# Layer 0's backward gates three feed-forward blocks later, and the last pass's second output half token block by token block

## The chip, the cores and the metric

One Trainium2 chip, eight of its cores. Each core runs the same program on one of the eight sequences of the batch; the cores exchange nothing. The time of a run is the device time of its slowest core in microseconds (us).

## The reference

A bidirectional encoder with two layers on x of shape 8 x 4096 x 1024, followed by a root-mean-square norm. Per layer:

```
h = rmsnorm(x); z = h @ w_in                       # u, v, lru_x, lru_gate, gate_A, gate_B
y_a = gelu(u) * (w_s @ layernorm(gelu(v)) + b_s)   # per chunk of 128 positions
xc  = conv4(lru_x)                                 # taps -1, 0, +1, +2
for each direction:                                # forward and backward
    r, i = sigmoid(xc @ w_r + b_r), sigmoid(xc @ w_i + b_i)   # 8 heads of 128 x 128
    a = sigmoid(L) ** (8 r);  h_t = a_t h_(t-1) + sqrt(1 - a_t^2) * i_t * xc_t
y_b = (h_fwd + h_bwd) * gelu(lru_gate)
x = x + (sigmoid(gate_A) * y_a + sigmoid(gate_B) * y_b) @ w_out
h = rmsnorm(x); g, u = split(h @ w_ffn_in)
x = x + (silu(g) * u) @ w_ffn_out                  # inner width 2816
```

## The kernel before, in words

The 4096 tokens are eight tiles of 512 tokens (`TT`), a tile is four blocks of 128 tokens (`NS`), the model width is eight blocks of 128 (`KC`), and the inner feed-forward width is 22 blocks of 128 (`FC`). Matrix products are in bf16 with 512 columns a matmul, sums in float32 PSUM. There are three passes over the tiles.

- **First pass**, tiles 0 to 7: layer 0's projections, gating branch and forward recurrence.
- **Second pass**, tiles 7 to 0: for tile j the rest of layer 0 (backward recurrence, merge, output projection, feed-forward), and in the same step, for tile j+1, the projections, the gating branch and the backward recurrence of layer 1.
- **Last pass**, tiles 0 to 7: the rest of layer 1 (forward recurrence, merge, output projection, feed-forward) and the final norm.

A step of the second pass goes over TensorE in this order: merge projections and layer 1's conv input; output projection; layer 1's v, u and gate_A projections with its eight gate pairs; then feed-forward input and output. The feed-forward input is 22 blocks, `("FI", f, 0)` and `("FI", f, 1)`, eight matmuls each (`ffn_in`, L1186). Between these blocks stand the eight gate pairs `("R0", c)` of layer 0's backward recurrence for the next tile (`gates`, L711: one matmul for r and one for i). The feed-forward output (`ffn_out`, L1208) is two halves of 512 output columns, `nb`. Each half needs six streamed weight chunks `q` of up to four rows of blocks, and four PSUM banks, one for each block `s` of 128 tokens.

What a gate pair needs: `xgates` casts the conv output `xm`, reloaded from HBM by `xcload` (L922 in layer 0, L908 in layer 1), to bf16 (`xcb`, L972, ScalarE). The product goes to one of the two PSUM banks of the ring "gate", and ScalarE's tanh writes it to `ra` or `ib` (L714). `xm`, `ra` and `ib` are single buffers of eight blocks for both layers. So layer 0's gates wait until layer 1's recurrence is through with them: `xm` may be loaded when L743 has read it, and `ib` may be written when the scans (L746) are done and `hbstore` (L914) has stored it to HB. Load and store are in two halves of four blocks, 1 MB each. `recur` then makes exp (L727), square (L733), square root (L738), product (L743) and scan.

Weights come from a bf16 copy WB in HBM in chunks of up to 512 KB (L1093) through a ring `wr` of 11 buffers. A chunk's buffer is free when its last matmul is done. All these DMAs are issued by SyncE (SPq in the rows), in its fixed order; an entry that waits holds up those behind it.

In the last pass the residual rows `xr` (512 KB for each 128 tokens) have a ring of five buffers, and a tile uses four. After `ffn_out` VectorE adds the product to `xr` (L1213), ScalarE squares it (L1547), GpSimd takes the root, VectorE scales it (L1551) and SyncE stores it to `out` (L1554). The next tile's output projection (L1162) adds to rows loaded by L1519 into the buffers so freed; the first of its four is free beforehand.

The order: TensorE's is written by hand (`seq`, lists of tokens, sorted by key). The order on the other engines is made by a list scheduler (`Sched.order`) from assumed costs and due times. So a moved token on TensorE also moves work elsewhere. PSUM banks are handed out in TensorE's order: five to "main", two to "gate", one to "t".

Of the kernel before, what the change touches and what calls it, by code (L numbers as in the profile page):

```python
# [14 lines left out]
KC = 8  # L15
# [5 lines left out]
NS = TT // 128  # L21
# [431 lines left out]
def build_program():  # L453
    nc = bass.Bass("TRN2", target_bir_lowering=False)
    stack = contextlib.ExitStack()
    with stack:
        _build(nc, stack)
    return nc
# [9 lines left out]
def _build(nc, stack):  # L468
# [819 lines left out]
    def seq(g, tokens):  # L1288
        return {t: (g, float(i)) for i, t in enumerate(tokens)}

    def fseq(extra):

        r = []
        for f in range(FC):
            r += [("FI", f, 0), ("FI", f, 1)] + [t for a, t in extra if a == f]
        return r + [("FO", nb, q, s) for nb in range(2) for q in range(6) for s in range(NS)]

    def aseq():
# [64 lines left out]
    for i in range(NT + 1):  # L1363
# [3 lines left out]
        tok = []  # L1367
# [22 lines left out]
        if j >= 0:  # L1390
            extra = [(n, t) for n, t in enumerate(late)]
            if i == 0:
                extra += [(2 + 2 * n, ("CON", n)) for n in range(5)]
            if j > 0:
                extra += [(int(7 + 1.7 * c), ("R0", c)) for c in range(KC)]
            tok += fseq(extra)
        else:
            tok += late
# [92 lines left out]
    for j in range(NT):  # L1491
        g = G3 + 1 + j
        nxt = j + 1 < NT
        tok = [("OP", s, nb) for s in range(NS) for nb in range(2)]
        extra = []
# [13 lines left out]
            tok += [("T2", s) for s in range(NS)]  # L1509
        if j + 2 < NT and j > 0:  # L1510
            extra += [(int(4 + 1.7 * c), ("R", c)) for c in range(KC)]
        tok += fseq(extra)
        if j == 0:
            for c in range(KC):
                tok.insert(tok.index(("FO", c // 6, c % 6, NS - 1)) + 1, ("R", c))
# [17 lines left out]
        for f in range(FC):  # L1533
            ffn_in(lambda t: K_["FI", f, t], hTb[0], hTb[1], sfi, f)
            if f in gat:
                c = gat[f]
# [45 lines left out]
```

How the kernel before makes its waits and increments, by code:

```python
            def body(eng, prog=self.prog[e], last=(self.final if e == "sp" else ())):  # L430
                for fn, waits, inc in prog:
                    for sem, v in waits:
                        eng.wait_ge(sem, v)
                    ins = fn(eng)
                    if inc is not None:
                        ins.then_inc(inc[0], inc[1])
                for sem, v in last:
                    eng.wait_ge(sem, v)
```

## Time and profile before

| | us |
|---|---|
| median of 3 runs | 4124.24 |
| the runs | 4122.54, 4124.24, 4664.74 |
| the profiled execution, its own time | 4136.46 |
| its span, core 1 (slowest) | 4134.9 |
| TensorE busy | 3747.6 (91%) |
| VectorE busy | 2467.1 (60%) |
| ScalarE busy | 2210.1 (53%) |

The profile is of one execution of its own, on core 1 unless another core is named. In timeline rows, the first number is the start in us from the beginning of the span, the second the time from the first start to the last end of the merged instructions, and in brackets stands the idle time of the engine before them and what ended it. A matmul of 512 columns starts every 0.216 us when nothing holds it up (64 in 13.8 us), though its row says 379 ns.

### The profile page before, as it was taken

To read this page: it belongs to the slowest core of one execution; us is meant where nothing else is said; L and a number is where in the kernel's file an instruction comes from. 1 tells how busy PE (TensorE), PEld (TensorE's weight loads), DVE (VectorE), ACT (ScalarE), POOL (GpSimd) and SP (SyncE) were. 2 spreads that over 40 slices of the span, in tenths; PEclk is the share of its full clock that TensorE was granted. 3 is DMA by queue.
4 is the path that set the end of the run, shared out by engine and by line. 5 is a ranking of instruction groups with operands and counts; after the bars stand their busy time and mean duration, and the time that the engine had idled before them with its cause. 6 is when DMAs were issued, how large, how long until landed. Compare 5 with 4: busy or idle time off the path is not lost.

```text
span 4134.9 us, 56456 instructions; the slowest of 8 cores (4063.2 to 4134.9 us)
## 1 busy us (share of the span) xinstructions
PE 3747.6 (91%) x17826; PEld 1706.4 (41%) x17826; DVE 2467.1 (60%) x3625; ACT 2210.1 (53%) x3252; POOL 350.3 (8%) x594
## 2 busy tenths in 40 slices
PE   5788888798999998999999999868999999999988
PEld 2333333343444444444444444323444444444443
DVE  4777777754657665665766666465565555645533
ACT  5777787743646547464645746485453443524211
POOL 3111111010100010010001000000000000000000
PEclk9888789899999999999999999988999999999999
DMA  9877778789787979878787776664667576575653
GB/s 197 150 143 135 138 158 179 223 163 244 214 223 235 233 246 220 257 207 231 225 231 246 226 243 196 202 212 145 210 230 236 184 235 208 198 249 158 199 166 102
DMA packets 368257, 836.92 MB, mean 202 GB/s; under 512 B 37264, under 2 KB 153184, under 8 KB 358880
## 3 DMA queue, kind: packets, MB, share of 16 engines
q1 hardware_dynamic: 252224, 767.25, 58.9%
q0 software_dynamic: 115744, 66.07, 14.2%
q8 instruction: 151, 2.47, 0.2%
q14 instruction: 138, 1.13, 0.1%
HBM read 748.27 MB, written 206.58 MB: 231 GB/s over the span
## 4 chain that ended last, share of the span: by engine, by line
PE 73%; DMA 11%; ACT 6%; issue 4%; DVE 4%; POOL 1%; SPq 0%; ACTq 0%; DVEq 0%; POOLq 0%
PE pfall L1186 26%; PE pfall L1004 17%; PE pfall L1208 14%; PE pfall L986 4%; PE pfall L1162 4%; PE pfall L956 3%; DMA HB<-ib 3%; PE pfall L1234 2%; DMA YA<-guth 2%; PE pfall L711 2%; DMA xs<-x 2%; DVE ib L746 1%; PE pfall L622 1%; DMA wzx<-w_in 1%; DMA xr<-XL 1%
## 5 line engine op out<-in xcount | busy, mean ns | idle before, releaser
L1186 PE MATMUL pfall<-hTa,wr 128*128 128x512 bf16 x2816 | 636.3, 385 | 5.4 <-ACT guth L1006 3.8
L1186 PE MATMUL pfall<-hTb,wr 128*128 128x512 bf16 x2816 | 621.0, 381 | 2.7 <-ACT hTb L1176 2.7
L1208 PE MATMUL pfall<-wr,ff 128*128 128x512 bf16 x2816 | 611.7, 379 | 0.0
L1004 PE MATMUL pfall<-hTa,wr 128*128 128x512 bf16 x1920 | 435.3, 382 | 2.0 <-ACT guth L1006 2.0
L1186 PEld LDWEIGHTS pfall<-hTa,wr 128*128 128x128 bf16 x2816 | 278.3, 99 | 345.6 <-issue 30.0
L1186 PEld LDWEIGHTS pfall<-hTb,wr 128*128 128x128 bf16 x2816 | 276.4, 98 | 338.1 <-issue 8.7
L1208 PEld LDWEIGHTS pfall<-wr,ff 128*128 128x128 bf16 x2816 | 275.5, 98 | 332.3
L1213 DVE SCALAR_TENSOR_TENSOR xr<-pfall,xr 128x512 f32<-128x512 f32 x128 | 79.5, 684 | 385.1 <-PE pfall L1208 385.1
L898 DVE SCALAR_TENSOR_TENSOR xm<-zb,cols,xm 128x512 f32<-128x512 f32 x384 | 277.2, 747 | 52.8 <-ACT hz L1241 20.8
L1162 PE MATMUL pfall<-wr,mT 128*128 128x512 bf16 x1024 | 239.8, 394 | 67.1 <-DVE mT L1151 42.7
L1004 PEld LDWEIGHTS pfall<-hTa,wr 128*128 128x128 bf16 x1920 | 187.3, 99 | 223.1 <-issue 12.2
L746 DVE TENSOR_TENSOR_SCAN ib<-ra,car,ib 128x512 f32<-128x512 f32 x224 | 277.4, 1270 | 0.9 <-DVE ib L743 0.5
L722 DVE SCALAR_TENSOR_TENSOR ib<-ib,xm 128x512 f32<-128x512 f32 x256 | 175.1, 688 | 152.0 <-ACT ib L714 150.9
L711 PE MATMUL pfall<-xcb,wg 128*128 128x512 bf16 x512 | 170.7, 404 | 93.1 <-ACT ib L714 50.7
L1006 ACT ACTIVATE bg<-pfall 128x512 f32<-128x512 f32 x240 | 141.8, 598 | 205.1 <-PE pfall L1004 183.3
L714 ACT ACTIVATE ra<-pfall,hbias 128x512 f32<-128x512 f32 x256 | 175.6, 686 | 141.7 <-PE pfall L711 139.1
L607 POOL TENSOR_SCALAR rs<-ss 128x1 f32<-128x1 f32 x160 | 50.7, 317 | 2235.2 <-ACT hb2a L1547 1047.5
L1004 PE MATMUL pfall<-h,wr 128*128 128x512 bf16 x1024 | 233.0, 381 | 6.4 <-ACT guth L1006 4.0
L743 DVE TENSOR_TENSOR ib<-ib,xm 128x512 f32<-128x512 f32 x256 | 165.0, 685 | 110.9 <-ACT xm L738 110.9
L1193 DVE SCALAR_TENSOR_TENSOR sg<-sg,pfall 128x512 f32<-128x512 f32 x176 | 119.0, 683 | 158.9 <-ACT sg L1191 158.4
L972 ACT CAST xcb<-xm 128x512 bf16<-128x512 f32 x256 | 153.2, 620 | 91.4 <-DMA xm<-XC 71.8
L727 ACT ACTIVATE ra<-ra,hcneg 128x512 f32<-128x512 f32 x256 | 197.3, 809 | 0.8
(167 smaller groups left out, 5178.7 us busy)
## 6 DMA issues: line engine op xcount, KB each, us to landing
wr<-WB SPq DMA_DIRECT2D x832, 512.0 KB, 5.2
XC<-xm SPq DMA_DIRECT2D x32, 1024.0 KB, 8.0
YA<-guth SPq DMA_DIRECT2D x128, 256.0 KB, 5.1
xm<-XC SPq DMA_DIRECT2D x32, 1024.0 KB, 9.1
ya<-YA SPq DMA_DIRECT2D x128, 256.0 KB, 6.3
WB<-w_ffn_in POOLq DMA_DIRECT2D x44, 512.0 KB, 13.6
WB<-w_in POOLq DMA_DIRECT2D x32, 512.0 KB, 31.2
HF<-ib SPq DMA_DIRECT2D x16, 1024.0 KB, 8.1
```

The lines of the kernel that those rows point to most:

```text
L711: sc.mm(key + (t,), p, [(lambda e, t=t, p=p: e.matmul(p.f(), lhsT=wg[:, t, c, :], rhs=xcb, start=True, stop=True), [bwg[t], bxcb])], MM)
L714: sc.op("act", lambda e, p=p, dst=dst, bc=bc: e.activation(out=dst[:, c, :], in_=p.f(), func=AF.Tanh, scale=0.5, bias=hbias[:, bc:bc + 1]) ...
L722: sc.op("dve", lambda e, c=c, x=x: e.scalar_tensor_tensor(out=ib[:, c, :], in0=ib[:, c, :], scalar=1.0, in1=x, op0=ALU.add, op1=ALU.mult), ...
L727: sc.op("act", lambda e, c=c, col=col: e.activation(out=ra[:, c, :], in_=ra[:, c, :], func=AF.Exp, scale=hcneg[:, col:col + 1], bias=hcneg ...
L743: sc.op("dve", lambda e, c=c, x=x: e.tensor_mul(out=ib[:, c, :], in0=ib[:, c, :], in1=x), 0.68, reads=[bib[c], bx], writes=[bib[c]])
L746: sc.op("dve", lambda e, c=c, rv=rv: e.tensor_tensor_scan(out=rv(ib, c), data0=rv(ra, c), data1=rv(ib, c), initial=(0.0 if first else pcar ...
L898: sc.op("dve", lambda e, k=k: e.scalar_tensor_tensor(out=x, in0=zb[:, k:k + TT], scalar=cols[:, k * 8 + c:k * 8 + c + 1], in1=x, op0=ALU.m ...
L986: sc.mm(keyf(s, nb), p, [(lambda e, k=k, s=s, w=w, p=p: e.matmul(p.f(), lhsT=hT[:, k, lo + s * 128:lo + (s + 1) * 128], rhs=w(k), start=(k ...
L1004: op = sc.mm(key, p, [(lambda e, k=k: e.matmul(p.f(), lhsT=w(k), rhs=hT[:, k, lo:lo + TT], start=(k == 0), stop=(k == KC - 1)), bh + [bw]) ...
L1162: sc.mm(keyf(s, nb), p, [(lambda e, k=k, s=s, w=w, p=p: e.matmul(p.f(), lhsT=mT[k][0][:, s * 128:(s + 1) * 128], rhs=w(k), start=(k == 0), ...
L1186: op = sc.mm(keyf(t), p, [(lambda e, k=k, o=o, q=q, p=p: e.matmul(p.f(), lhsT=q[:, k, o:o + 128], rhs=hT[:, k, 0:TT], start=(k == 0), stop ...
L1208: sc.mm(keyf(nb, q, s), ps[s], [(lambda e, f=f, s=s, t=t, q=q, p=ps[s]: e.matmul(p.f(), lhsT=fs[f][0][:, s * 128:(s + 1) * 128], rhs=t[:, ...
```

## The change

Two edits. In the second pass the gate pair c of layer 0 stands after feed-forward block 10 + 3c//2 (10, 11, 13, 14, 16, 17, 19, 20) and no longer after int(7 + 1.7c) (7, 8, 10, 12, 13, 15, 17, 18). In the last pass the second half of `ffn_out` (nb = 1) goes block by block over the tokens: all 22 matmuls of s = 0, then of s = 1, and so on. The first half, and both halves in the second pass, stay with the weight chunk outside and the four token blocks inside.

```diff
-    def fseq(extra):
+    def fseq(extra, last=False):
+
 
         r = []
         for f in range(FC):
             r += [("FI", f, 0), ("FI", f, 1)] + [t for a, t in extra if a == f]
+        if last:
+            r += [("FO", 0, q, s) for q in range(6) for s in range(NS)]
+            return r + [("FO", 1, q, s) for s in range(NS) for q in range(6)]
         return r + [("FO", nb, q, s) for nb in range(2) for q in range(6) for s in range(NS)]
...
             if j > 0:
-                extra += [(int(7 + 1.7 * c), ("R0", c)) for c in range(KC)]
+                extra += [(10 + 3 * c // 2, ("R0", c)) for c in range(KC)]
             tok += fseq(extra)
...
         if j + 2 < NT and j > 0:
             extra += [(int(4 + 1.7 * c), ("R", c)) for c in range(KC)]
-        tok += fseq(extra)
+        tok += fseq(extra, True)
```

The first tile of the last pass also has gate pairs `("R", c)` inside its feed-forward output: each stands behind `("FO", c // 6, c % 6, NS - 1)`. With the second half in the new order, the pairs of c = 6 and 7 come behind the first and second chunk of its last token block.

How this moves instructions, first on TensorE, in the feed-forward input of a step of the second pass (wr is a weight chunk, xcb the cast input of a gate pair). Here and below, lines with - are the order before, with + the new one:

```order
 L1186 MATMUL pfall<-hTa_184,wr_107_151 128x512 x8
-L711 MATMUL pfall<-xcb_165_209,wg_112_156 128x512 x2
 L1186 MATMUL pfall<-hTa_184,wr_108_152 128x512 x8
 L1186 MATMUL pfall<-hTa_184,wr_109_153 128x512 x8
-L711 MATMUL pfall<-xcb_166_210,wg_112_156 128x512 x2
 L1186 MATMUL pfall<-hTa_184,wr_108_152 128x512 x8
 L1186 MATMUL pfall<-hTa_184,wr_109_153 128x512 x8
 L1186 MATMUL pfall<-hTa_184,wr_110_154 128x512 x8
 L1186 MATMUL pfall<-hTa_184,wr_100_144 128x512 x8
-L711 MATMUL pfall<-xcb_167_211,wg_112_156 128x512 x2
+L711 MATMUL pfall<-xcb_165_209,wg_112_156 128x512 x2
```

The first gate pair (xcb_165) stands three blocks, that is 48 matmuls, later. One block lies between the first and the second pair as before.

On SyncE's queue, at the same place, the load of the first half of xm and the store of the first half of ib to HB:

```order
 L1093 DMA wr_103_147<-WB 128x2048
+L1093 DMA wr_104_148<-WB 128x2048
 L922 DMA xm_111_155<-XC 128x2048
-L1093 DMA wr_104_148<-WB 128x2048
 L1093 DMA wr_105_149<-WB 128x2048
 L914 DMA HB<-ib_132 128x4x512
```

The xm load now stands behind one more weight chunk. The second HB store, further down, stands behind two more.

On SyncE's queue, between the last two tiles of the last pass (out and XL are the stores and loads of the residual rows xr). Before:

```order
L1093 DMA wr_110_154<-WB 128x2048
L1093 DMA wr_100_144<-WB 128x2048
L1554 DMA out<-xr_637_681 128x1024
L1554 DMA out<-xr_633_677 128x1024
L1554 DMA out<-xr_634_678 128x1024
L1519 DMA xr_637_681<-XL 128x1024
L1554 DMA out<-xr_635_679 128x1024
L1519 DMA xr_633_677<-XL 128x1024
L1519 DMA xr_634_678<-XL 128x1024
```

With the change:

```order
L1093 DMA wr_105_149<-WB 128x2048
L1558 DMA out<-xr_637_681 128x1024
L1523 DMA xr_637_681<-XL 128x1024
L1558 DMA out<-xr_633_677 128x1024
L1093 DMA wr_106_150<-WB 128x2048
L1093 DMA wr_107_151<-WB 128x2048
L1093 DMA wr_108_152<-WB 128x2048
L1093 DMA wr_109_153<-WB 128x2048
L1093 DMA wr_110_154<-WB 128x2048
L1558 DMA out<-xr_634_678 128x1024
L1523 DMA xr_633_677<-XL 128x1024
L1093 DMA wr_100_144<-WB 128x2048
```

Two stores and the first load now stand ahead of six weight chunks (wr_106 to wr_100) that stood ahead of them all.

## Rows read from the trace of the kernel before

**Rows 1.** Head of the page: the slowest core's span and the spread of the cores.

```profile
span 4134.9 us, 56456 instructions; the slowest of 8 cores (4063.2 to 4134.9 us)
```

**Rows 2.** Waits of TensorE, core 1, whole span: total us, times, longest.

```profile
PE pfall L711 <- ACT ib L714: 50.7, 30, 5.9
PE pfall L711 <- ACT xcb L972: 30.9, 9, 7.7
PE pfall L1162 <- DVE xr L1165: 23.7, 7, 5.5
```

**Rows 3.** The same of core 7.

```profile
PE pfall L711 <- ACT xcb L972: 4.8, 6, 1.4
```

**Rows 4.** Chain that ended last, in order of time: the feed-forward outputs that bound the steps.

```profile
1190.14 37.99 PE pfall L1208 x176
...
2372.54 37.99 PE pfall L1208 x176
...
2594.63 36.71 PE pfall L1208 x170
...
3114.45 36.71 PE pfall L1208 x170
...
3936.68 36.71 PE pfall L1208 x170
```

**Rows 5.** Timeline of TensorE, core 1, first gate pairs of a second-pass step.

```profile
1610.69 1.01 PE L711 MATMUL pfall<-xcb,wg 128*128 128x512 bf16 x2 [7.75 <-ACT xcb L972]
1611.49 5.88 PE L1186 MATMUL pfall<-hTa,wr 128*128 128x512 bf16 x16
...
1620.92 0.38 PE L711 MATMUL pfall<-xcb,wg 128*128 128x512 bf16 x1 [3.33 <-ACT ib L714]
```

**Rows 6.** Timeline of SyncE's queue, core 1, same step: load of xm, store to HB.

```profile
1591.34 0.32 SPq L922 DMA_DIRECT2D xm<-XC  x1
1594.38 2.05 SPq L1093 DMA_DIRECT2D wr<-WB  x2
1597.99 0.37 SPq L914 DMA_DIRECT2D HB<-ib  x1
```

**Rows 7.** Timeline of ScalarE, core 1, same step: the cast, and the first write of ib.

```profile
1609.92 0.62 ACT L972 CAST xcb<-xm 128x512 bf16<-128x512 f32 x1 [11.83 <-DMA xm<-XC]
...
1620.09 0.69 ACT L714 ACTIVATE ib<-pfall,hbias 128x512 f32<-128x512 f32 x1 [1.62 <-DMA HB<-ib]
```

**Rows 8.** The HB store and that write on core 7, same step.

```profile
1558.36 0.37 SPq L914 DMA_DIRECT2D HB<-ib  x1
...
1571.12 0.69 ACT L714 ACTIVATE ib<-pfall,hbias 128x512 f32<-128x512 f32 x1 [1.37 <-DMA HB<-ib]
```

**Rows 9.** Stretch of core 1: length, busy us of PE, PEld, DVE, ACT, POOL, clock, DMA share, GB/s.

```profile
1600.00:1610.00 10.00, 2.94 (x14) 1.15 (x12) 2.10 (x4) 0.07 (x1) 0.84 (x1) 0.79 1.00 224
```

**Rows 10.** Timeline of VectorE, core 1: last scans, then the additions of the first output half.

```profile
1681.88 2.45 DVE L746 TENSOR_TENSOR_SCAN ib<-ra,car,ib 128x512 f32<-128x512 f32 x2
...
1686.58 2.48 DVE L1213 SCALAR_TENSOR_TENSOR xr<-pfall,xr 128x512 f32<-128x512 f32 x4 [2.25 <-PE pfall L1208]
```

**Rows 11.** Timeline, core 1, between two tiles of the last pass: TensorE, SyncE's queue, VectorE.

```profile
3499.34 2.74 PE L1162 MATMUL pfall<-wr,mT 128*128 128x512 bf16 x8 [3.62 <-DVE xr L1165]
...
3492.95 0.33 SPq L1519 DMA_DIRECT2D xr<-XL  x1
...
3498.50 0.69 DVE L1165 SCALAR_TENSOR_TENSOR xr<-pfall,xr 128x512 f32<-128x512 f32 x1 [3.19 <-DMA xr<-XL]
```

**Rows 12.** Timeline of TensorE, core 1, last tile: output projection to feed-forward input.

```profile
3974.50 12.25 PE L1162 MATMUL pfall<-wr,mT 128*128 128x512 bf16 x56
...
4004.33 7.97 PE L1186 MATMUL pfall<-hTb,wr 128*128 128x512 bf16 x26 [1.35 <-ACT hTb L1176]
```

**Rows 13.** Timeline, core 1, end of the program: VectorE's additions, the first store.

```profile
4119.46 2.48 DVE L1213 SCALAR_TENSOR_TENSOR xr<-pfall,xr 128x512 f32<-128x512 f32 x4 [16.51 <-PE pfall L1208]
...
4124.25 5.78 SPq L1554 DMA_DIRECT2D out<-xr  x4
```

## The prediction

> **What bounds the kernel now.** I began with the head of the page: core 1 is the slowest at 4134.9 us, and the cores spread down to 4063.2 [rows 1]. The table of times gives the profiled execution itself 4136.5 us, and TensorE 91% busy. What the change can give lies in TensorE's idle time, plus the slow clock behind it. So I read TensorE's waits next. Three lines concern the places the change touches [rows 2]: gate pairs waiting for ScalarE to write ib (50.7 us, 30 times), gate pairs waiting for the cast (30.9 us), and the output projection waiting for VectorE's addition to the residual rows (23.7 us, 7 times). On core 7, the fastest, the cast costs only 4.8 us [rows 3]. So the cores differ in how late their transfers land.
>
> Then the chain in order of time, for the length of a step [rows 4]. From one feed-forward output to the next, five steps of the second pass take 2372.54 - 1190.14 = 1182.4 us, 236.5 each. The step behind them, which has no gate pairs of layer 0, takes 222.1. Sixteen gate matmuls at 0.216 us are 3.5 us, so a step without waits would take 225.6, and the five lose 54 us together, 10.9 each.
>
> The timelines show how. In a step at 1600 us the xm load is issued at 1591.34 [rows 6] and the cast that needs it starts at 1609.92 [rows 7]. TensorE has waited 7.75 us at the first gate pair [rows 5]. It then runs 16 feed-forward matmuls in 5.88 us, where 3.5 is their pace (granted clock 0.79 in this stretch [rows 9], so part of it at the lower level, 1.2 GHz), and waits 3.33 us more for a gate bank. That bank is held by the tanh that writes ib, and it is held because the HB store issued at 1597.99 [rows 6] has landed only by 1620.09 [rows 7]. The waits and the slow clock make 7.75 + 3.33 + about 2.3 = 13.4 us in this step. ScalarE and VectorE are no bound there: busy for 0.07 and 2.10 us of ten [rows 9].
>
> **Part one: the gate pairs, three blocks later.** No instruction is added, removed or resized. Work put ahead of the first pair: 48 matmuls x 0.216 = 10.4 us. That cover is real work, which needs only weights from a ring 11 deep; TensorE has no wait for a weight chunk in this pass. The queue takes something back. The xm load now stands behind one more chunk, issued in the row at 1594.38 [rows 6], so it leaves about 3.3 us later; with the 18.6 us that it took, it lands at about 1613.2. The first pair without any wait stood at 1610.69 - 7.75 = 1602.9 and now stands at 1613.3. So the 7.75 us go, give or take half a microsecond.
>
> The HB store decides the rest. Its place among the transfers does not change, but all four scans ahead of it now stand behind one more feed-forward product (L1197), for which I take 1.1 us. If it takes its 22.1 us again, ib may be written at 1621.2 and the bank is free at about 1622.0. Without waits, the second pair's second matmul would have come at 1620.92 - 3.33 - 7.75 - 2.3 = 1607.5, and now at 1617.9. A wait of 4.1 us stays, and the step gains 13.4 - 4.1 = 9.3 us. That is the cap wherever the loss is larger. Where it is smaller, the whole of it goes. On an average loss of 10.9 with some steps well below it, I take 8 us for a step. There are six such steps with a full feed-forward ahead of them (the step before the first row of the chain is the sixth), so 48 us. The first of the seven steps with these pairs has hardly a wait, and I give it nothing. Bounds: above, the whole loss, 54 + 12 = 66 us; below, a fast core's, where the store lands 12.8 us after its issue [rows 8] and the losses are small anyway: about 4.5 us a step, 27.
>
> For the store's duration the Trainium skill speaks another way: its page "HBM Reference", section Specifications (TRN2), gives each core about 358 GB/s with both cores of a pair busy, by which 1 MB takes, as an estimate, 2.9 us, no wait would stay, and this part would come to its upper bound. The trace does not agree: 22.1 us, in a stretch with 224 GB/s and a DMA share of 1.00 [rows 9].
>
> What is late next: the recurrence. The last pair moves from block 18 to block 20, 7 us nearer to the end of the input. The last scans then move by about as much past the start of the feed-forward output. VectorE's order now has six of the eight products and scans of that half ahead of the first half's additions (L1213) and two scans behind them. Before, the scans ended at 1684.3 and the additions waited 2.25 us for TensorE [rows 10]. Adding up the ScalarE and VectorE operations from the new place of the pair, I get the last work ahead of the additions done at about 1685.3, 1.3 us before they are due. So it costs nothing, narrowly. The merge that uses these scans comes 20 us later.
>
> **Part two: token block by token block.** The matmuls are the same 88, so TensorE's own time does not change. The first three token blocks finish 14.2, 9.5 and 4.7 us earlier. Now all four additions come together, the store of a block follows 4.8 us behind its addition (as at the program's end, 4119.46 to 4124.25 [rows 13]), and the first reload is issued at 3492.95, 9.5 us after the next output projection began; VectorE waits for it until 3498.50 and TensorE 3.62 us [rows 11]. With the change the first store leaves about 9.5 us before the projection, the reload 4 us before it, and it lands 1 to 3 us into it; it is due at 7. The second and third land at about 9 and 14 us and are due at 10.4 and 13.8, with four further PSUM banks of slack. All these waits should go.
>
> Price: five tiles take 3936.68 - 3114.45 = 822.2 us [rows 4]. Their work is 720 matmuls of 512 columns at 0.216, 1.8 us of transposes, and 3.5 us of gate pairs in four of them: 800.5. They lose 22 us, waits and slow clock. The border behind the first tile has the longest wait, 5.5 us [rows 2], with the clock about 7. Together 29; I take 27, as gate pairs of that first tile move 11 us later. The last tile: from the start of its projection to its feed-forward input 4004.33 - 3974.50 = 29.8 us [rows 12], of which 13.8 are the projection. The norm and transposes of the last token block alone need about 8 behind it, so 29.8 - 21.8 = 8 at most, and I take 6. The end: the last addition starts 1.8 us after 4119.46, its store 4.8 later, at 4126.1; the last of the four stores was issued at about 4129.7 [rows 13]: 3.6 us. Sum 27 + 6 + 4 = 37. Bounds: 41 above; 12 below, if the loads stay late and only the tail and part of the last tile gain.
>
> The other cost: the six weight chunks of this half are now freed within its last 4.7 us instead of over 19 us, and SyncE meets them between stores and loads. The earliest to be needed of those that follow is due some 15 us into the next tile, issued 4 us before it: 19 us of slack. The nearest rows are for 1 MB, twice its size: 12.8 us on core 7 and 22.1 on core 1 [rows 6 to 8]. I take nothing.
>
> **The sum**: 48 + 37 = 85 us, 4136.5 - 85 = 4051 against the profiled execution. It was 12 us above the median of the runs; if its excess is plain slowness, the median goes to 4124.2 - 85 = 4039, and if it lay in these very waits, to 4051. I take 4046.
>
> **The rivals.**
> - *The lateness goes with the waits* (chance 0.20). If transfers are late because TensorE's stall bunches them (DMA share 1.00 while it stands [rows 9]), they land earlier and both parts reach their upper bounds: 66 + 41 = 107, 4017 to 4030. For it: core 7 has the same program and half the latency. Against it: the bytes of a step are the same, in less time.
> - *The stretch is bound by transfers* (0.18). Then the HB store lands later by most of what TensorE gains, and the second pass gives 20 us in place of 48: 57 in all, 4067 to 4079. For it: share 1.00 at only 224 GB/s. Against it: core 7 moves the same bytes in shorter steps. The Trainium skill's "HBM Reference", section Specifications (TRN2), says that a pair shares one domain, so one core's earlier demand would slow the other's.
> - *The reloads stay late* (0.09): burst and stores compete, part two gives 12: 60 in all, 4064 to 4076.
> - *VectorE's order bites* (0.05): the additions of the first half are held behind L743, which waits for the square root. It decides once the recurrence is over 1.3 us later than I summed. At 3 us a step, seven times, 21 us go back: 4060 to 4072.
> - *Slower* (0.03): the weight burst. A chunk for the next tile that lands more than 19 us after its issue stalls TensorE at each of seven borders. To turn the gain over it must cost 12 us at each, so a load of 31 us; the HB store's 22.1 us on core 1 shows that 19 can be passed, but in a stretch fuller than this one. Then 4124 to 4140.
> - That the change does not do what it says is excluded for the order; whether the cores' slowest is core 1 again is open, and costs at most the 12 us above.
>
> **Chances and range.** The forecast case, 4034 to 4060, has 0.45. A measurement here can tell about 2%, that is 82 us, or 4041.8. Below that lies the first rival and two fifths of the forecast case: faster 0.38. Slower 0.03, within 2% 0.59. Range 4018 to 4085.
>
> **What would show it.** Right: no cast wait over 2 us at the gate pairs in the second pass on any core; an ib wait of 2 to 5 us left on the slowest and none on the fastest; steps of 228 to 230 us on core 1; tiles of the last pass 4 us shorter with no wait of L1162 for L1165; stores spaced 4.7 us apart; the last addition to the end of the span shorter by 3 to 4 us. Wrong: steps still over 233 us, a new wait of L1208 for L1213 in the second pass, or waits for weight chunks behind the projection.

## The result, and the profile after

| | before | with the change |
|---|---|---|
| median, us | 4130.6 (4 runs) | 4081.17 (4 runs, 4078.02 to 4460.88) |
| profiled execution, its own time, us | 4136.46 | 4080.89 |

The ratio is 0.9885, with a 95% interval of 0.9861 to 0.991: about 47 us less, where I had forecast 85 (against the profiled execution) and a time of 4046. The range of 4018 to 4085 holds the time. By the bound of 2% this is "within", which I gave 0.59. Medians over all runs include some in which one die ran at a lower clock; ratios, and the runs and cores compared below, leave these out.

Head of the page after, which answers to [rows 1]:

```profile
span 4079.3 us, 56449 instructions; the slowest of 8 cores (4020.1 to 4079.3 us)
```

The slowest core is now core 4, and it is core 4 below. Its waits of TensorE (total us, times, longest), against [rows 2]:

```profile
PE pfall L1186 <- DVE sg L1193: 34.7, 5, 13.0
PE pfall L711 <- ACT ib L714: 32.0, 28, 4.0
...
PE pfall L1004 <- DVE xr L1165: 7.1, 6, 1.3
PE pfall L622 <- DVE hb2b L617: 6.4, 2, 4.8
PE pfall L711 <- ACT xcb L972: 3.4, 4, 0.9
```

Of core 7, the fastest, against [rows 3]:

```profile
PE pfall L711 <- ACT xcb L972: 3.2, 4, 0.9
PE pfall L1186 <- DVE sg L1193: 2.4, 1, 2.4
```

The two waits that I meant to remove are gone. Of the cast's 30.9 us only 3.4 are left, in four waits of at most 0.9 us, none of them at the gate pairs that moved; and the output projection's 23.7 us for the residual rows are gone on every core. The first line is new: the feed-forward input waits for VectorE's product with the tanh. It is as large as the one that went, and it stands on the slower core of each pair, 28.0 to 34.7 us on cores 0, 3, 4 and 6, against 2.4 to 5.3 on the others.

The chain that ended last gives the lengths of the steps, against [rows 4] (start, us, feed-forward output):

```profile
930.84 36.71 PE pfall L1208 x170
1188.71 36.71 PE pfall L1208 x170
...
2345.93 37.99 PE pfall L1208 x176
2567.01 36.71 PE pfall L1208 x170
...
3081.82 37.99 PE pfall L1208 x176
...
3888.89 37.99 PE pfall L1208 x176
```

| stretch (rows 4 and the fence above) | before | after | gain |
|---|---|---|---|
| five steps of the second pass | 1182.4 | 1157.2 | 25.2 |
| the step behind them | 222.1 | 221.1 | 1.0 |
| from there to the end of the last pass's first tile | 519.8 | 514.8 | 5.0 |
| five tiles of the last pass | 822.2 | 807.1 | 15.1 |
| from the last chain row to the end of the span | 198.2 | 190.4 | 7.8 |

The rest of the 55.6 us between the two spans, 1.5, lies ahead of 1190 us. So a step on the slow core shrank from 236.5 to 231.4 us, where my expectation was 228 to 230, and the sixth step (930.84 to 1188.71) took 257.9 us, where it had taken 258.6 (its row before follows). It holds the longest of the new waits, the 13.0 us.

```profile
931.52 38.00 PE pfall L1208 x176
```

Now the step at 1600 us, which answers to [rows 5 to 7]. TensorE:

```profile
1593.64 3.40 PE L1186 MATMUL pfall<-hTa,wr 128*128 128x512 bf16 x15
1603.50 7.73 PE L1186 MATMUL pfall<-hTa,wr 128*128 128x512 bf16 x24 [6.46 <-DVE sg L1193]
1611.07 0.60 PE L711 MATMUL pfall<-xcb,wg 128*128 128x512 bf16 x2
```

ScalarE:

```profile
1587.01 1.08 ACT L1191 ACTIVATE sg<-pfall 128x512 f32<-128x512 f32 x2
1601.10 0.62 ACT L972 CAST xcb<-xm 128x512 bf16<-128x512 f32 x1 [13.00 <-DMA xm<-XC]
1601.62 0.59 ACT L1191 ACTIVATE sg<-pfall 128x512 f32<-128x512 f32 x1
```

VectorE, and SyncE's queue:

```profile
1602.67 0.69 DVE L1193 SCALAR_TENSOR_TENSOR sg<-sg,pfall 128x512 f32<-128x512 f32 x1 [11.86 <-ACT sg L1191]
```

```profile
1583.72 0.56 SPq L922 DMA_DIRECT2D xm<-XC  x1
...
1587.91 0.37 SPq L914 DMA_DIRECT2D HB<-ib  x1
```

Read them from the gate pair backwards. The pair at 1611.07 doesn't wait for its cast, as forecast. But the cast stands in ScalarE's order ahead of a tanh of the feed-forward, and it waits 13.00 us for the load issued at 1583.72. ScalarE takes its instructions in order, so the tanh behind it (1601.62) waits too, and with it VectorE's product (11.86 us idle). A feed-forward block holds two of the five "main" banks until that product is done. TensorE therefore goes on for about five banks of eight matmuls (5 x 8 x 0.216 = 8.6 us, from about 1588 to 1603.50 - 6.46 = 1597.04) and then stops for 6.46 us. After it, 24 matmuls take 7.73 us where 5.2 are their pace. The loss in this step is 6.46 + 2.5 = 9.0 us, where it had been 13.4. The wait for ib at these pairs is gone too: in the six steps TensorE waited there 27.5 us for casts and 21.8 us for ib before (core 1), and for neither now (core 4). Core 7, the fastest, had 1.6 and 22.2 us there, and has 0.7 left besides its 2.4 us at L1186; its steps went from 229.9 us to 225.0, to the 225.6 that I had put for a step without waits.

The border between two tiles of the last pass, against [rows 11]: TensorE, VectorE, SyncE's queue.

```profile
3302.21 5.34 PE L1004 MATMUL pfall<-hTa,wr 128*128 128x512 bf16 x24 [1.30 <-DVE xr L1165]
```

```profile
3299.97 0.69 DVE L1146 SCALAR_TENSOR_TENSOR bg<-bg,bg 128x512 f32<-128x512 f32 x1 [4.13 <-ACT bg L1006]
3300.76 0.69 DVE L1149 TENSOR_TENSOR hf<-hf,bg 128x512 f32<-128x512 f32 x1
3301.37 0.69 DVE L1165 SCALAR_TENSOR_TENSOR xr<-pfall,xr 128x512 f32<-128x512 f32 x1
```

```profile
3282.03 0.60 SPq L1558 DMA_DIRECT2D out<-xr  x1
...
3286.58 0.34 SPq L1558 DMA_DIRECT2D out<-xr  x1
3291.24 0.32 SPq L1523 DMA_DIRECT2D xr<-XL  x1
```

The output projection (L1162) does not wait for the residual rows any more, but each of six borders has this new wait of 1.3 us. The projection began at 3281.74; the last reload it needs leaves at 3291.24 (the four of a border land 4.9 to 11.4 us after their issue). But the addition at 3301.37 doesn't wait for it in the row: it stands in VectorE's order behind two operations of the next merge, and the first of these waits 4.13 us for ScalarE. The reload had landed 6.6 us after its issue, at 3297.8, 3.5 us ahead of the addition. And the line in the list of waits (7.1 us, six times, 1.3 at most) is the same on all eight cores, early and late ones, as a fixed order makes it and late transfers hardly would. The last tile, against [rows 12]:

```profile
3926.71 13.98 PE L1162 MATMUL pfall<-wr,mT 128*128 128x512 bf16 x64
...
3951.43 1.01 PE L622 MATMUL pfall<-ident_b,hb2b 128*128 128x128 bf16 x8 [4.79 <-DVE hb2b L617]
3954.07 6.21 PE L1186 MATMUL pfall<-hTb,wr 128*128 128x512 bf16 x22 [1.63 <-ACT hTb L1176]
```

From the start of its projection to its feed-forward input it takes 27.4 us, before 29.8. And the end of the program, against [rows 13]:

```profile
4060.22 14.22 SPq L1558 DMA_DIRECT2D out<-xr  x4
```

```profile
4069.60 0.69 DVE L1213 SCALAR_TENSOR_TENSOR xr<-pfall,xr 128x512 f32<-128x512 f32 x1 [0.32 <-PE pfall L1208]
```

The last addition starts 9.7 us before the end of the span, where it was 13.6 (4119.46 + 1.8 to 4134.9): 3.9 us, as I had said, and the four stores start 4.6 us apart in the mean (14.22 less the 0.33 of the last issue, by 3).

### The profile page after: what moved, and what is told of

It is laid out like the page before. It is cut to its first block, busy times and chain, and to the rows that moved or that the text cites. A ratio compares the mean times of both kernels' runs of the same rounds, so it can differ in the third digit from the quotient of the medians.

```text
span 4079.3 us, 56449 instructions; the slowest of 8 cores (4020.1 to 4079.3 us)
## 1 busy us (share of the span) xinstructions
PE 3695.2 (91%) x17826; PEld 1693.6 (42%) x17826; DVE 2473.2 (61%) x3625; ACT 2209.3 (54%) x3252; POOL 333.9 (8%) x594
## 3 DMA queue, kind: packets, MB, share of 16 engines
q0 software_dynamic: 115744, 66.07, 14.5%
## 4 chain that ended last, share of the span: by engine, by line
PE 75%; DMA 10%; ACT 6%; issue 4%; DVE 3%; POOL 0%; SPq 0%; ACTq 0%; DVEq 0%; POOLq 0%
PE pfall L1186 28%; PE pfall L1004 16%; PE pfall L1208 15%; PE pfall L1162 5%; PE pfall L986 3%; PE pfall L1234 2%; DMA YA<-guth 2%; PE pfall L711 2%; DMA xm<-XC 2%; PE pfall L956 2%; DMA xs<-x 2%; DMA wzx<-w_in 1%; PE pfall L622 1%; DMA hf<-HF 1%; ACT guth L1006 1%
## 5 line engine op out<-in xcount | busy, mean ns | idle before, releaser
L1186 PE MATMUL pfall<-hTa,wr 128*128 128x512 bf16 x2816 | 634.1, 385 | 39.9 <-DVE sg L1193 34.7
L1186 PE MATMUL pfall<-hTb,wr 128*128 128x512 bf16 x2816 | 621.2, 381 | 3.0 <-ACT hTb L1176 3.0
L1004 PE MATMUL pfall<-hTa,wr 128*128 128x512 bf16 x1920 | 434.8, 382 | 9.1 <-DVE xr L1165 7.1
L1186 PEld LDWEIGHTS pfall<-hTa,wr 128*128 128x128 bf16 x2816 | 277.0, 99 | 378.0 <-issue 60.0
L1186 PEld LDWEIGHTS pfall<-hTb,wr 128*128 128x128 bf16 x2816 | 276.4, 98 | 338.5 <-issue 9.0
L1004 PEld LDWEIGHTS pfall<-hTa,wr 128*128 128x128 bf16 x1920 | 186.3, 98 | 229.4 <-issue 18.1
L1162 PE MATMUL pfall<-wr,mT 128*128 128x512 bf16 x1024 | 230.4, 385 | 45.7 <-DVE mT L1151 40.0
L1213 DVE SCALAR_TENSOR_TENSOR xr<-pfall,xr 128x512 f32<-128x512 f32 x128 | 81.7, 685 | 280.9 <-PE pfall L1208 280.9
L1004 PE MATMUL pfall<-h,wr 128*128 128x512 bf16 x1024 | 234.7, 383 | 5.6 <-ACT guth L1006 3.2
```

The lines of the kernel that those rows point to most:

```text
L1004: op = sc.mm(key, p, [(lambda e, k=k: e.matmul(p.f(), lhsT=w(k), rhs=hT[:, k, lo:lo + TT], start=(k == 0), stop=(k == KC - 1)), bh + [bw]) ...
L1162: sc.mm(keyf(s, nb), p, [(lambda e, k=k, s=s, w=w, p=p: e.matmul(p.f(), lhsT=mT[k][0][:, s * 128:(s + 1) * 128], rhs=w(k), start=(k == 0), ...
L1186: op = sc.mm(keyf(t), p, [(lambda e, k=k, o=o, q=q, p=p: e.matmul(p.f(), lhsT=q[:, k, o:o + 128], rhs=hT[:, k, 0:TT], start=(k == 0), stop ...
```

## The experiments

The question was where the 38 us between 85 and 47 are. My theory (Q): the stall of the first part moved from the gate pairs to the tanh, through the order of ScalarE's queue. The rival (D): the stretch is bound by its transfers, and whatever is taken off one wait comes back in another. Each ratio below is to the kernel before, timed beside the experiment on the same chip.

**The first part alone.** The change without its second edit:

```
-        tok += fseq(extra, True)
+        tok += fseq(extra)
```

> The gate pairs moved, the last pass left as before. Theory Q (the stall moved into ScalarE's queue: its cast of xm stands ahead of the tanh of feed-forward blocks, so a late xm load now stops TensorE at L1186 instead of at L711): about 20 to 30 us below the kernel before, with a wait of L1186 for L1193 of 5 to 13 us in some steps of the slower cores and none on the faster ones; no change after the second pass. Theory D (the stretch is bound by transfers): the same total, but the wait stands at the gate pairs (L711, for ib or for the cast), not at L1186. If the two parts of the change add up, this one and the token order alone together give the 49 us of the whole.

Ratio 0.9928 (0.9896 to 0.996), 29.6 us of 4115: far from the 48 forecast, near the lower bound of 27. The new wait belongs to this part, and its old companion is gone: on core 1, as theory Q had it,

```profile
PE pfall L1186 <- DVE sg L1193: 23.9, 5, 5.7
```

and 20.4 us on core 2, but 3.7 us on core 0 and none on core 3. The gate pairs that moved don't wait for their casts there.

**The second part alone.**

```
-                extra += [(10 + 3 * c // 2, ("R0", c)) for c in range(KC)]
+                extra += [(int(7 + 1.7 * c), ("R0", c)) for c in range(KC)]
```

> The second output half of the last pass token block by token block, the gate pairs left as before. From the two traces: core 4 went from 1184 to 1165 us between the first feed-forward output of the last pass and the end, so 19 us, and core 1 would have had 27: 17 to 28 us below the kernel before. My prediction's 37 would need five tiles 4.4 us shorter each and the tail 4 us shorter. Waits of L1162 for L1165 gone, second pass unchanged.

Ratio 0.9954 (0.993 to 0.9978), 19 us, where the prediction had 37 and this expectation 17 to 28. Its waits, core 6, the slowest:

```profile
PE pfall L711 <- ACT xcb L972: 23.7, 8, 7.4
...
PE pfall L1004 <- DVE xr L1165: 7.1, 6, 1.3
```

The 1.3 us waits belong to this part, the cast's are those of before. 0.72% and 0.46% are 1.18%, and the whole gave 1.15%: the parts add up within their intervals, and both fell short.

**The change with the casts held back.** ScalarE's order puts the cast c of layer 0's second-pass gates behind TensorE's feed-forward block that stands before its gate pair; the rest is as in the change:

```
+    def xgates(l, d, xm, wg, bwg, keyf, hold=lambda c: None):
...
+            sc.op("act", ..., tset="copy", after=hold(c))
...
+            rgates(0, 1, j - 1, wgb0, lambda c: K_["R0", c],
+                   lambda c: K_["FI", min(10 + 3 * c // 2, FC - 1), 0])
```

> The whole change, and in the second pass each cast of xm for layer 0's gates is ordered on ScalarE not before the feed-forward block just ahead of its gate pair. Theory Q: the wait of L1186 for L1193 goes on every core, a wait of up to 5 us at L711 stays on the slower cores, steps there 226 to 230 us instead of 229 to 235, and the time is 12 to 25 us below the change's, 4056 to 4069. Theory D: the wait comes back at L711 with the same length, time within 5 us of the change's.

Ratio 0.9841 (0.9799 to 0.9883), two runs of 4053.8 and 4056.2 us. Its waits on core 2, the slowest, have no line of L1187 (L1186 before) for sg at all:

```profile
PE pfall L711 <- ACT ib L714: 38.6, 31, 6.0
PE pfall L711 <- ACT xcb L972: 11.0, 6, 6.7
```

Chain and timeline of the same core:

```profile
923.50 36.71 PE pfall L1209 x170
1176.70 37.99 PE pfall L1209 x176
...
2317.33 37.99 PE pfall L1209 x176
```

```profile
1582.05 0.60 ACT L1192 ACTIVATE sg<-pfall 128x512 f32<-128x512 f32 x1 [2.86 <-PE pfall L1187]
1585.72 0.62 ACT L972 CAST xcb<-xm 128x512 bf16<-128x512 f32 x1 [3.07 <-DMA xm<-XC]
```

The load takes as long as in the change (17.1 us from issue to landing against 17.3), and the cast still waits for it, but only 3.07 us, and the tanhs stand ahead of it. Five steps now take 1140.6 us, 228.1 each. Before they took 1182.4: 41.8 us less, and the sixth step is 253.2 (before 258.6), 5.4 less. Together 47.2 us, where the prediction had 48 for this part. The ratios say much the same, with wide intervals: 65 us in all, less the 19 of the second part, is 46. In the six steps, what TensorE waits for casts and ib at the moved pairs and for sg at the feed-forward blocks among them was 49.3 us before (core 1), 34.7 with the change (core 4), and is 16.7 now (core 2). So Q stands, and D falls as it was put: the same bytes are moved, and the waits don't come back. The first part was right in size once the cast no longer blocks ScalarE.

D's premise is not empty, though. With the casts held the store to HB lands later, 16.9 to 18.8 us after its issue in the median on the late cores 1, 2, 4 and 6, where the late cores of the change have 13.6 to 14.5; and the loads of xm in these steps have a median of 19.3 us on core 2 against 11.2 on core 4 of the change. The shorter step pays part of its gain back in slower transfers. What is left of it as waiting is most of the 16.7 us: one cast of 6.7 us, over the 5 us expected, and waits for ib of 2.76 and 5.96.

**Casts held, gates at their old places** (with the second part).

> Token order as in the change, gate pairs at their old places, casts held as in the run before this. Theory Q: with the pairs early nothing useful stands behind the cast, so holding it gives nothing: the same time as the token order alone within 6 us, waits for the cast at L711 as before (about 30 us on the slower cores). Theory D expects the same; the run only excludes that holding the casts is a gain by itself.

Ratio 0.9946 (0.9916 to 0.9977), no different from the second part alone (0.9954), and its cast wait on core 0 is the old one:

```profile
PE pfall L711 <- ACT xcb L972: 23.3, 9, 6.6
```

Holding the casts alone gives nothing, since TensorE has nothing to do meanwhile; moving the gates alone gives part of the gain, since ScalarE can't serve the work that stands there.

**The planner told of the load.** The casts have no place written by hand; the planner's duration for these loads is 14 us longer:

```
-               XHALF, reads=[bXC[j][h]], writes=...
+               XHALF, slow=14.0, reads=[bXC[j][h]], writes=...
```

> The whole change, with no place of a cast written by hand: the planner is told that these two loads take 14 us longer than its model says, and so sets the casts itself where ScalarE would have nothing to wait for. Theory Q: L1186 <- sg under 5 us, and the time that of the kernel with the casts held, 4050 to 4062 us (ratio 0.983 to 0.986). Rival P (the longer estimate also moves other instructions, as copies of the carry and the scans, behind work they are needed before): 4065 to 4090, with new waits of PE at the step's end.

Ratio 0.9861 (0.9835 to 0.9886), 4048.2 to 4066.6 us; no sg wait on core 4, the slowest, and 11.0 us for casts in ten waits of at most 2.1. The sg wait is gone from all cores, and P's time, 4065 and more, was met by one run of five. So the cause lies in the estimate by which the order was made, not in the casts as such. It is a little behind the order set by hand, within what the intervals tell.

**A quarter of the load's bytes, in as many pieces.** The reloads fetch 128 of 512 tokens:

```
+        n = TT if j == NT - 1 else TT // 4
-        ... out=xm.group(h), in_=XC[j, :, 4 * h:4 * h + 4, :]
+        ... out=xm.group(h)[:, :, 0:n], in_=XC[j, :, 4 * h:4 * h + 4, 0:n]
```

> The whole change, but the reloads of the convolution's output for layer 0's backward gates fetch 128 of the 512 tokens (0.25 instead of 1 MB each; all but those of the first backward step), so these gates are computed partly from old data; nothing else differs. It asks whether the lateness of these two 1 MB loads is what still stops the slow cores at the tanh of the feed-forward blocks (34.7 us of L1186 <- sg on core 4 of the changed kernel). Theory Q (the late load holds the cast, the cast heads ScalarE's queue): with a quarter of the bytes the casts start some 7 to 10 us earlier, the waits L1186 <- sg fall under 8 us, and what is left of L711 <- ib shrinks by the part that follows late casts; the time is 4045 to 4062 us, ratio 0.980 to 0.986. Theory D (the stretch is bound by the sum of what is moved): 12 MB less of some 300 MB over the span would be worth about as much, 4050 to 4070, but with the waits merely moved; it is told from Q by the waits, which under D stay over 20 us in sum at this place. If the load's start (queued behind weight chunks and the store of h) and not its length is what is late, the waits stay at 25 to 35 us and the time at 4075 to 4085.

Ratio 0.9853 (0.9815 to 0.989), 4056.3 to 4058.8, inside Q's range and D's. (The loads left out are 14 x 0.75 = 10.5 MB; a core moves 837 MB over its span.) The waits for sg fell to 15.6 us in 4 on core 5, the slowest, and to 16.8 to 20.4 on the other late cores, but not under 8, which is what Q as I had put it asked for; D's sum of over 20 stands on one core of the four. The load and its cast there:

```profile
1570.25 0.65 SPq L923 DMA_DIRECT2D xm<-XC  x1
```

```profile
1585.74 0.62 ACT L973 CAST xcb<-xm 128x512 bf16<-128x512 f32 x1 [11.11 <-DMA xm<-XC]
```

15.5 us for 0.25 MB, where the whole 1 MB took 17.4 in the step above (1583.72 to 1601.10). The twelve such loads of the six steps (the window 1000 to 2400 us), first with the change on core 4, then here on core 5:

```profile
DMA to landing us min/median/max: 6.6/11.2/24.2
```

```profile
DMA to landing us min/median/max: 4.5/9.3/15.4
```

So three quarters of the bytes are worth about 2 us of 11 in the median; over all cores the medians are 9.2 to 12.0 us with the change and 6.9 to 9.7 here. The lateness is mostly not the load's own size. The Trainium skill ("DMA: Bandwidth & Descriptors", section Anatomy of one DMA — SWDGE (gpsimd) path) gives about 2.0 us plus the bytes over 436 GB/s, for another issuing path: by it, as estimates, 4.4 us for 1 MB and 2.6 for a quarter. Neither the 17.4 nor the 15.5 agrees; the difference of the medians, about 2 us, is near that of the two estimates.

**A quarter in a quarter of the pieces.** Only one of each four blocks of 128 rows is fetched:

```
+        n = 4 if j == NT - 1 else 1
-        ... out=xm.group(h), in_=XC[j, :, 4 * h:4 * h + 4, :]
+        ... out=xm.group(h)[:, 0:n, :], in_=XC[j, :, 4 * h:4 * h + n, :]
```

> The whole change, but of layer 0's backward reloads only the first of the four 128-row blocks of each half is fetched (128 rows of 2 KB, 0.25 MB; all but those of the first backward step), so these gates are computed partly from old data. The run before it fetched as many bytes in four times as many pieces (512 rows of 512 B) and its loads took 8.9 us in the median, no less than the 7.6 us of the full 1 MB, and up to 15.5 us on a late core. Theory P (the number of pieces, not of bytes, sets what such a load takes): median 3 to 5 us, L1186 <- sg under 8 us on every core, 4045 to 4058 us. Theory B (what stands ahead of it in the queue and the partner core's traffic set it): again 7 to 10 us in the median and 12 or more on the core of each pair that comes second; L1186 <- sg 12 to 20 us there, 4052 to 4065 us. For both: in each of the four pairs the core that reaches the first feed-forward output of the second pass later is the one that then takes more time for its steps.

One run, 4068.8 us, where the kernel before has 4110.3 to 4127.1 on that chip. The same loads on core 5:

```profile
DMA to landing us min/median/max: 4.5/11.3/16.9
```

The waits for sg are 13.8 to 19.5 us on the late cores 1, 2, 5 and 6, as theory B had them, and the medians of the loads on these cores are 8.7 to 11.3 us, no shorter than in as many bytes and more pieces (8.9 to 9.7), but under the 12 us that B put there; the one time is 4 us over B's range. So P falls: it is not the pieces either. What is left is what is under way when the load is issued: the core's own store and weight chunks, and the partner core's traffic. The runs don't separate these two.

**Gates later still**, after blocks 11, 12, 13, 15, 16, 18, 19, 21, casts held:

```
+                extra += [(11 + 10 * c // 7, ("R0", c)) for c in range(KC)]
```

> The casts held back, and layer 0's gate pairs and their casts put later still, after feed-forward blocks 11, 12, 13, 15, 16, 18, 19, 21 instead of 10, 11, 13, 14, 16, 17, 19, 20. With the casts held, L711 <- xcb keeps 11.0 us (6 waits) and L711 <- ib 38.6 us (31 waits) on core 2. Theory Q: about 8 us more cover for the two loads takes 6 to 10 us of L711 <- xcb away, and the closer end of the gates leaves L711 <- ib and the recurrence as they are: 4044 to 4052. Rival E (the gates now end too late: scans, products and the next step's store and first conv wait): 4056 to 4075, with waits of PE for VectorE behind the feed-forward. Rival N: what is left is not from late loads, 4052 to 4058.

4046.4 to 4048.6 us, ratio 0.983 (0.98 to 0.986); the cast wait of core 6, the slowest, is 6.5 us in place of 11.0: 4.5 us less, where Q expected 6 to 10, though the time is in its range. Against the ratio with the casts held, 0.9841, the intervals show no difference.

**A sixth buffer for residual rows in the last pass**, paid with one of eleven weight buffers, casts held:

```
-    WRN = 11
+    WRN = 10
...
-    xr5 = Ring([... 60 * K, QX + 26 * K])])
+    xr5 = Ring([... 60 * K, QX + 26 * K, 40 * K])])
```

> The whole change with the casts held back (ratio 0.9841, 4054 to 4056 us), a sixth buffer for the residual rows of the last pass, paid with one of the eleven weight buffers. The last pass shows two new waits: 1.3 us of PE at L1004 <- xr L1165 at each of 6 borders (the fourth reload of the residual waits for a store), and 4.8 us at L622 <- hb2b near its end. Theory R (the fifth buffer's release through the store is their cause): the L1004 waits go, 6 x 1.3 = 8 us, and the time is 4042 to 4050. Rival W (the eleventh weight buffer hides late weight chunks): weight loads come later by one chunk (1.5 to 2 us of cover), waits of PE for weights show up, 4054 to 4075. Rival N (the wait is for VectorE's add, which comes late in any case): 4051 to 4057, no change.

4043.2 to 4059.7 us, ratio 0.9838 (0.9813 to 0.9862), no better than with the casts held alone (0.9841). On core 2, the slowest, the lines of L1004 for xr and of L622 for hb2b are gone (line numbers are one higher here, L1005), and tiles take 160.6 us in place of 162.1. With the buffer free early, the planner also sets the last additions ahead of the merge (below), so the run shows that the two together are the cause, and not which. But the seventh step takes 229 us where 221 were, which takes most of the gain back, as rival W had it. Its wait isn't for weights, though, but for a merge input:

```profile
2398.61 15.15 PE L1163 MATMUL pfall<-wr,mT 128*128 128x512 bf16 x56 [4.83 <-DVE mT L1152]
```

**Both of the last two edits**, with ten weight buffers only from the last pass on:

```
+    wring = Ring(wring.items[:10])
```

> Casts held, gate pairs still later (after blocks 11 to 21), and the sixth residual buffer of the last pass paid with the eleventh weight buffer only from the last pass on, so that the two middle passes keep all eleven. The kernel with casts held and gates still later took 4046.4 to 4048.6; in the one with six residual buffers and ten weight buffers throughout, the last pass's tiles took 160.6 instead of 162.0 us, but each step of the third stage's end lost up to 6 us to weight chunks. Theory R (the buffer's release is the cause of the 1.3 us waits, the ring of ten costs only in the middle passes): L1004 <- xr gone, tiles of 160.6 us, the time 4046 to 4048 less 6 x 1.3 and 2 to 4 at the last tile, 4034 to 4040, ratio 0.979 to 0.982. Rival W (ten weight buffers cost in the last pass as well, as seen at its start): 4042 to 4052.

4036.4, 4036.8 and 4068.6 us beside 4107.3 to 4130.3 of the kernel before; ratio 0.9847 (0.973 to 0.9964), wide since these are only three runs. The seventh step takes 221.1 to 222.9 us on the eight cores, where the run before had 227.4 to 229.0: what was lost there is the price of ten weight buffers in the middle passes. Core 6, the slowest of the profiled one, last tile:

```profile
3884.98 13.98 PE L1163 MATMUL pfall<-wr,mT 128*128 128x512 bf16 x63
...
3909.31 6.07 PE L1187 MATMUL pfall<-hTb,wr 128*128 128x512 bf16 x19 [1.74 <-ACT hTb L1177]
```

24.3 us, where the change takes 27.4. VectorE at its first border, the last addition now ahead of the merge:

```profile
3259.96 0.69 DVE L1166 SCALAR_TENSOR_TENSOR xr<-pfall,xr 128x512 f32<-128x512 f32 x1 [1.03 <-PE pfall L1163]
3264.10 0.69 DVE L1147 SCALAR_TENSOR_TENSOR bg<-bg,bg 128x512 f32<-128x512 f32 x1 [3.45 <-ACT bg L1007]
```

Two of three runs lie in the 4034 to 4040 of theory R, the third lies 28 us above it; that it is the best of all is not settled by this interval.

**The change once more**, on the chip of the last one:

> The change as it is, timed again beside the others on one chip. Every theory expects what was measured: 4075 to 4085 us, a ratio to the kernel before of 0.986 to 0.991, and on the cores that run late 25 to 35 us of PE waits at L1186 <- sg, on the others under 5.

4065.2, 4071.7 and 4085.0 us, ratio 0.9899 (0.9836 to 0.9962). On cores 4 and 6 of the profiled run the sg waits are 25.5 and 23.4 us, at the lower end of the 25 to 35 expected and a little under it, and on cores 5 and 7 they are 3.4 and 2.2. Against it, the two lower runs of the kernel above are 29 to 49 us faster; its third is as slow as the change.

## Why the prediction was right and wrong

**The range held, and the forecast did not.** 4081 lies within 4018 to 4085, but outside the forecast case (4034 to 4060) and outside the bands of all rivals. None of them had the wait that came. That the range held the time is owed to its width.

**The waits named were the right ones.** Both edits took away what they were to take: no cast wait over 0.9 us, no wait of L1162 for L1165, on any core. The reading that idle TensorE time in these places was worth tens of microseconds held. On the fast cores part one came out as its lower bound said (4.5 us a step; core 7 went from 229.9 to 225.0).

**The step that failed in part one** is "That cover is real work, which needs only weights from a ring 11 deep". A feed-forward block also needs two PSUM banks, and gets them back only through ScalarE's tanh and VectorE's product. ScalarE's queue had the cast that waits for the load in front of that tanh, since the planner thought the load short (told of 14 us more, it made an order without this wait). So TensorE could run 8.6 us ahead on its banks and no further, whatever work stood in front of the pair. The part gave 29.6 us alone; with the casts held the slowest core's six steps became 47.2 us shorter, and 48 was the forecast. The row was there: in [rows 7] ScalarE idles 11.83 us in front of the cast, and I read it only for the cast's time. The Trainium skill has the rule ("PSUM — Partial Sum Buffer", section Engine vs sequencer instructions: the queues of ScalarE, VectorE and GpSimd are strict FIFO), and the row at 1601.62, a tanh right behind the cast that had waited 13.00 us, agrees. "ScalarE and VectorE are no bound there" rested on their busy time; a queue whose head waits is a bound at 0.07 us busy.

**The cap of 9.3 us a step and the HB store** could not be tested as put, since the wait came earlier. In the kernel with casts held the moved pairs do wait for ib, 2.76 us in the step where I had 4.1, 5.96 in one other, and 0.2 or nothing in the remaining four.

**Part two was over-sized, and the step that failed is** "All these waits should go". I had followed the reloads to their landing, and not VectorE's order behind them, where the last additions stand behind the merge. That is the same mistake as in part one, on another engine. Five tiles were to lose nothing and lose 807.1 - 800.5 = 6.6 us, which is 5 x 1.3 and a little. The forecast for them and the first border was 27; the five tiles gained 15.1 and the stretch with the first tile 5.0. The last tile was to give 6 and gave 2.4 (4.79 us of wait at hb2b are left); with a sixth buffer it gives 5.5. The tail was to give 4 and gave 3.9. Besides, the 22 us were read off core 1, whose waits for the residual rows were the longest of all cores. On the rows of the two profiles the last pass and its end gain 5.0 + 15.1 + 7.8 = 27.9 us; timed alone, over several executions, part two is worth 19.

**What was said to cost nothing cost nothing.** VectorE's order at L1213 bit nowhere, and no matmul of the feed-forward output waited for it; TensorE waited for no weight chunk in the last pass, so the rival that ends slower did not appear.

**The rivals.** The time, 4081, lies beside the band of "the stretch is bound by transfers" (4067 to 4079), but the same transfers run in 4054 when ScalarE's order is mended. Its mechanism was not what the change met: the HB store did not land later in the median, 13.7 us on core 4 where core 1 had 13.3 before. It does show, at a smaller price, once the steps get short: with the casts held the store takes 17.7 us on core 2. "The lateness goes with the waits" falls by its time (4017 to 4030) and not by its mechanism: on the late cores the loads of xm in the six steps took 16.2 to 19.3 us in the median before and take 11.2 to 12.0 with the change. But the longest still take up to 26.1, and the one at 1583.72, behind which TensorE stops, took 17.4; with the casts held the medians are back at 19.3 to 19.8. Why they fell and rose is open.

## What to carry to other kernels

When you move work so that it covers a wait, follow it through every engine that has to finish it, and ask what stands in front of it in each in-order queue; an idle engine may be idle because its head waits, and then it can't serve the cover. Move the waiting instruction back together with its consumer, or give the planner the duration that the trace shows under load. When a transfer lands in time, look whether the instruction that uses it stands in time as well.

## What the runs showed of the hardware

**Which core is slow is settled within each pair.** In both profiles, before and after, the core of a pair (0 and 1, 2 and 3, 4 and 5, 6 and 7) that reaches the first feed-forward output of the second pass later ends up with the longer span, in all eight pairs. Before, these were cores 1, 2, 4 and 6, after it 0, 3, 4 and 6. The head start is 5 to 11 us, as here on cores 4 and 5 with the change:

```profile
930.67 3.62 PE L1208 MATMUL pfall<-wr,ff 128*128 128x512 bf16 x16
```

```profile
923.33 2.97 PE L1208 MATMUL pfall<-wr,ff 128*128 128x512 bf16 x13
```

Core 5, 7.3 us ahead here, took 225 us a step and ended at 4037.1 us; core 4 ended at 4079.3. The profiles of all eleven experiments show it too, in every pair. It is an observation: that the partner's traffic delays the second core's loads fits it, and no run held a partner still.

**A load's time was mostly not set by its size.** 15.5 us for 0.25 MB on a core that comes second and 17.4 for 1 MB. Over the twelve loads at the same places the medians are 9.2 to 12.0 us for 1 MB on the eight cores of the change, and 6.9 to 9.7 for 0.25 MB, so four times the bytes are worth 2 to 3 us. With the casts held, the same 1 MB loads have 19.3 to 19.8 us on the late cores and 11.9 to 14.7 on the others.
